# One table of order numbers changed, and 128 transposes of a hybrid GLA / DeltaNet / MLA block written as matrix products

## The reference

```python
g_cum = jnp.cumsum(g, axis=2)
g_h = jnp.swapaxes(g_cum, 2, 3)
incl = jnp.tril(jnp.ones((C, C), dtype=bool))
diff = g_h[..., :, None] - g_h[..., None, :]
decay = jnp.where(incl, jnp.exp(jnp.where(incl, diff, 0.0)), 0.0)
l_strict = jnp.where(strict, jnp.einsum('bnthd,bnshd->bnhts', k_beta, k) * decay, 0.0)
t_inv = lax.linalg.triangular_solve(eye + l_strict, ..., left_side=True, lower=True, unit_diagonal=True)
```

## Time and profile before

| what | value |
|---|---|
| median of three runs | 2180.62 us |
| profiled execution, its own time | 2180.62 us |
| its span (first to last instruction) | 2178.7 us |
| PE busy | 2109.8 us, 97% of the span |
| PEld, DVE, ACT, POOL busy | 1439.6, 927.1, 841.6, 294.7 us |
| mean granted PE clock | 0.991 |

### The profile page before, as it was taken

How to read it: one execution, slowest core, us unless ns; L and a number is a source line. 1 busy time by engine, 2 the same in 40 slices (tenths; PEclk the granted TensorE clock), 3 DMA queues, 4 the chain that set the end, 5 groups by cost and what they waited for, 6 DMA issues and landing times. The chain is left out here.

```text
span 2178.7 us, 31299 instructions
## 1 busy us (share of the span) xinstructions
PE 2109.8 (97%) x10890; PEld 1439.6 (66%) x10890; DVE 927.1 (43%) x2293; ACT 841.6 (39%) x2203; POOL 294.7 (14%) x623
## 2 busy tenths in 40 slices
PE   8999999999989999999999999999989979999998
PEld 5667576656556886555674446776676668976687
DVE  3023554857563235443231111246677653343321
ACT  1223354645443234444231112246556443245420
POOL 1000006153350000000000000000632641000000
PEclk9999999999999999999999999999999999999999
DMA  8326303221311022111122332231422312332333
GB/s 271 105 73 195 118 22 109 65 68 43 100 40 49 26 88 79 60 50 44 63 77 78 116 99 101 77 100 41 134 79 74 97 55 78 108 100 85 112 129 122
DMA packets 192443, 192.31 MB, mean 88 GB/s; under 512 B 28943, under 2 KB 186467, under 8 KB 191779
## 3 DMA queue, kind: packets, MB, share of 16 engines
q1 hardware_dynamic: 186048, 171.08, 25.4%
q0 software_dynamic: 4672, 18.89, 2.8%
q10 hardware_dynamic: 1571, 0.34, 0.1%
HBM read 180.78 MB, written 9.50 MB: 87 GB/s over the span
## 5 line engine op out<-in xcount | busy, mean ns | idle before, releaser
L1153 PE MATMUL bank<-hT,ring 128*128 128x512 f32 (+2 forms) x1856 | 715.1, 533 | 5.6 <-ACT hT L1557 3.6
L1153 PEld LDWEIGHTS bank<-hT,ring 128*128 128x128 f32 (+1 forms) x1856 | 331.7, 189 | 257.1 <-issue 239.1
L1153 PE MATMUL bank<-ring,hT 128*128 128x256 f32 (+2 forms) x2112 | 449.8, 368 | 0.0
L1153 PE MATMUL bank<-WORK 128*128 128x128 f32 (+6 forms) x3056 | 392.0, 286 | 37.3 <-DVE O L2202 13.3
L1153 PEld LDWEIGHTS bank<-ring,hT 128*128 128x128 f32 x2112 | 380.4, 190 | 62.4 <-issue 17.2
L1153 PEld LDWEIGHTS bank<-WORK 128*128 128x128 f32 (+4 forms) x3056 | 320.5, 170 | 144.9 <-issue 123.3
L1153 PE MATMUL bank<-yT,ring 128*128 128x512 f32 (+1 forms) x768 | 270.2, 489 | 0.0
L1153 PEld LDWEIGHTS bank<-yT,ring 128*128 128x128 f32 x768 | 139.2, 191 | 78.7 <-issue 69.7
L2126 DVE SCALAR_TENSOR_TENSOR WORK<-WORK,CW 128x512 f32<-128x512 f32 (+1 forms) x192 | 142.1, 740 | 2.2
L1512 ACT ACTIVATE E<-bank 128x512 f32<-128x512 f32 (+1 forms) x84 | 45.0, 536 | 207.4 <-PE bank L1153 198.2
L1116 POOL TENSOR_TENSOR WORK<-WORK 128x126 f32<-128x126 f32 (+22 forms) x248 | 107.3, 432 | 19.4
(11 more groups left out here) (215 smaller groups left out, 2009.6 us busy)
## 6 DMA issues: line engine op xcount, KB each, us to landing
ring<-in_w_in_dram SPq DMA_DIRECT2D x92, 1024.0 KB, 5.3
ring<-in_w_branch_dram SPq DMA_DIRECT2D x24, 1024.0 KB, 5.1
ring<-in_ada_w_dram SPq DMA_DIRECT2D x18, 1024.0 KB, 7.1
ring<-in_w_out_dram SPq DMA_DIRECT2D x8, 1024.0 KB, 5.1
WORK<-in_ada_w_dram SPq DMA_DIRECT2D x6, 1024.0 KB, 12.6
ring<-in_mla_q_up_dram SPq DMA_DIRECT2D x8, 576.0 KB, 4.1
xs<-yT POOLq DMA_DIRECT2D x2, 2048.0 KB, 7.5
WORK<-LD POOLq DMA_DIRECT2D x16, 256.0 KB, 3.4
```

What stands on the lines that cost most here:

```text
L1153: return nc.tensor.matmul(o, a, b, start=start, stop=stop, skip_group_check=True)
```

## The change

Two edits. The table `AHEAD` has other numbers and fewer kinds: `ga` 1 to 2, `cv` 6 to 5, `go` -4 to -3, `dn` -3 to -1, `abT` -3 to -7, `dw2` -5 to 3, `vz` 4 to 1, `gqk` -1 to 1; and `norm` -2, `vdsilu` -1, `dg` -12, `ge` -1, `dgp` -2 and `out` 1 are gone, which makes them 0.

In `d1`, PE no longer transposes a broadcast column of the running sums `GC` against the identity. It multiplies a broadcast column of `GG` (the log decays before they are summed) with the triangular table, which sums them on the way. The four results, their bank, what reads them and what `d1` waits for stay.

```diff
-AHEAD = {('yT', 1, 0): 0, 'gw': 4, 'ga': 1, 'dnq': 1, 'yT': -1, 'cv': 6, 'ms': 1, 'mkv': 6, 'muk': -6, 'dx6': 3, 'dqkv': 5, 'd1': -1, 'muq': 2, 'dya': 2, 'vdn': -1, 'gv': 4, 'ab': 4, 'go': -4, 'dn': -3, 'mo': -8, 'vdsil2': 0, 'abT': -3, 'sq': -3, 'nx': 3, 'dy6': 3, 'dv': 1, 'dyb': 2, 'mod': 6, 'gatt': -6, 'gx': -4, 'z2': -4, 'sk': -1, 'dw2': -5, 'modT': -2, 'dw': 1, 'd3': 1, 'gb': -2, 'vz': 4, 'lr': -3, 'mqT': 3, 'vgate': -4, 'gqk': -1, 'dsilu': -2, 'norm': -2, 'vdsilu': -1, 'dg': -12, 'ge': -1, 'dgp': -2, 'out': 1}
+AHEAD = {('yT', 1, 0): 0, 'gw': 4, 'ga': 2, 'dnq': 1, 'yT': -1, 'cv': 5, 'ms': 1, 'mkv': 6, 'muk': -6, 'dx6': 3, 'dqkv': 5, 'd1': -1, 'muq': 2, 'dya': 2, 'vdn': -1, 'gv': 4, 'ab': 4, 'go': -3, 'dn': -1, 'mo': -8, 'vdsil2': 0, 'abT': -7, 'sq': -3, 'nx': 3, 'dy6': 3, 'dv': 1, 'dyb': 2, 'mod': 6, 'gatt': -6, 'gx': -4, 'z2': -4, 'sk': -1, 'dw2': 3, 'modT': -2, 'dw': 1, 'd3': 1, 'gb': -2, 'vz': 1, 'lr': -3, 'mqT': 3, 'vgate': -4, 'gqk': 1, 'dsilu': -2}
...
                     for r in range(2):
                         for hh in range(2):
                             u = 2 * r + hh
-                            ins = tr(ps[:, u * P:(u + 1) * P], col(GC, tt, g, u).broadcast_to([P, P]))
+                            ins = mm(ps[:, u * P:(u + 1) * P],
+                                     col(GG, tt, g, u).broadcast_to([P, P]), kc(C_TRI + r * P))
```

## The result

The changed kernel takes 2193.68 us (median of 4 runs, 2192.64 to 2197.02) against 2181.02 us of the kernel before on the same chip (4 runs, 2179.77 to 2182.47). The ratio is 1.0056, 95% interval 1.0043 to 1.0069: 12.2 us slower, 9.4 to 15.0. One run of the kernel before, beside the last experiment, took 4456.07 us and is left out of that ratio. The time forecast was 2188.0, the range 2178 to 2197. The time is in the range and the direction was the likeliest one, but it lies 1.7 us above the upper end of the forecast alone.

A forecast was written before the change was run, and what follows sets the result against it. PE, busy 97% of the span, was taken to bound the kernel. Passes left on the path 8.6, `dw2` -1.2, GLA and `dg` +1.0, rest 0, clock -1.0 make +7.4 on 2180.6: 2188.0 us, range 2178 to 2197.

The forecast's parts named there:

- the forecast alone: Whole kernel: the main forecast without its rivals, 2184.5 to 2192 us, chance 0.56.
- The size of the new `d1`: PE in `d1`: 128 transposes become two-row products of 0.222 us instead of 0.109, adding 14.5 us in all.
- Rival 4: PE in `d1`: a product takes one pass, so the edit costs PE nothing; 2179.4 us, chance 0.04.
- What is hidden: PE holes at the `d2` and `dx`: 5.9 us of added passes are free, 8.6 stay; bounds 4 and 14.5.
- the first clock term: Two half-clock windows behind PE holes: shorter holes bring less time at 1.2 GHz, -1.0 us; bounds -3.8 and +1.7.
- `dw2` earlier: PE's `dy6` of group 2: waits of 1.18 and 2.07 us for ACT go, layer 1's gain is given back; -1.2 us.
- The last square and sum of the layer change stand as they did: Layer change: moving `out` and `norm` leaves these behind the last `out`, at no cost; bounds -2 and +2 us.
- GLA and `dg`: GLA part: `dg` and the gate entries stand closer to their producers, +1.0 us; bounds -1 and +5.
- the third window: Half-clock stretch before the `dx` of (1,3), 8.43 us of PE busy: POOL's landing decides there, so it gives nothing.
- rival 2: `dg` and `ge`: the order costs more, DVE late for `dgp` once per layer plus half clock; 2197 us, chance 0.15.
- Rival 1: DeltaNet groups: POOL's solve or DVE's chain decides in every group, so all 14.5 us fall into holes; 2175.6 us, chance 0.11.
- Rival 3: PE's clock holds behind the first two windows and one more place, 3 to 4 us back; about 2185 us, chance 0.14.

The follow-up runs named there:

- the last experiment: Kernel before with `dw2` early for group 2 alone and 20 gate and `ys` pieces pulled ahead of one `d2` and three `dx`: 2178.19 us, ratio 0.9982.
- the halves of the heads: Two kernels, each the kernel before with the new `d1` in four of the eight heads, with holes or mostly without: 2182.18 and 2188.14 us.
- the early heads: Kernel before with the new `d1` only in heads (0,0), (0,1), (0,2) and (1,0): 2188.14 us, ratio 1.0029.

## Why the prediction was right, and where it was not

1. *The size of the new `d1`.* Right: 128 more rows, 0.222 us for a product, 14.5 us of passes. The rule in the Trainium skill ("TensorE: Matmul & The Clock Gate", section Terms: the transpose mode is four times faster for float32), by which it would have been 41.9 us, does not hold in this kernel. Rival 4 (one pass) is dead.
2. *What is hidden.* Right, and shown: the holes at the `d2` of (0,1), (1,2) and (1,3) went, those of (0,3), (1,1) and the `dx` of group 2 shrank by 0.9 to 1.5 us with the new `d1` alone, and the halves of the heads cost 1.1 and 6.3 us where the count gave 1.8 and 6.5 to 6.8. One bound doesn't come out of its own words: two more hidden pairs, those of (0,2) and (1,0), leave 8.6 - 1.8 = 6.8 us, not 4. With the first clock term the forecast for the new `d1` was 7.6 us; 6.1 was measured.
3. *`dw2` earlier.* The step that failed. The prediction said -1.2 us, bounds 0 and -3.3; alone it is +4.4. It worked out group 2, where -1.5 us was measured (-3.3 to +0.4), and gave that for an entry that moves the copies in all eight groups. The question to ask was what else the copies now stand ahead of on ACT: in groups 0 and 1 of layer 1 that is `dd`, on which the next head's DVE rows wait, and `dyb`. In the changed kernel the two `dy6` wait only 1.06 and 0.70 us, so the entry's share of the 12.2 us is likely smaller than 4.4; it was not measured well enough to say (2.6 us, with overlapping intervals). The give-back at the `dx` of (1,3) was right: 3.94 us with group 2 alone, and 6.01 in the changed kernel, where PE's half clock just ahead of it is 5.00 us instead of 8.48, which brings it another 1.7 us earlier.
4. *"The last square and sum of the layer change stand as they did".* Wrong: PE waits 1.47 us for ACT's square there, and with the two entries back it doesn't. The prediction put this term at 0. What it costs in time is not shown apart from `dw2` and `dn`.
5. *GLA and `dg`.* Taken +1.0, found -0.4 with the rest of the table, with an error of some 3 us. No wait at `dg`. The working was right: between the end of `dgp` and the row that reads `dg` there are 4.7 us now instead of 9. That row still waits, for ACT, and nothing on PE does:
```profile
1475.08 0.22 DVE L2102 SCALAR_TENSOR_TENSOR WORK<-WORK 128x64 f32<-128x64 f32 x1
...
1479.98 0.23 DVE L2106 COPY WORK<-bank 128x64 f32<-128x64 f32 x1 [1.64 <-ACT WORK L1708]
```
6. *The clock.* Taken -1.0, for the first two windows of the earlier trace rows; not shown. With the new `d1` alone PE's half clock behind those two holes is 5.99 and 3.41 us, more in sum than before; in the changed kernel it is 3.41 and none. Such stretches can't be read off one profile: between two executions of one kernel the clock moves the time by more than 1 us (below). That the third window gives nothing was right, as the new `d1` alone showed.
7. *The rivals.* The measured time lies between the forecast and rival 2, 2197, "the order costs more". It is nearer to rival 2 (3.3 us) than to the forecast (5.7). That rival's headline was true, but not its place: it had `dg` and `ge`, which never waited. Rival 1 (the solve paces more than two groups) is excluded by the early heads, which paid for 6.3 of 7.3 us. Rival 3 was right that the clock holds more: its mean rose from 0.9904 (20 runs) to 0.9927 (10) with the new `d1` alone, and to 0.9919 in the changed kernel. Its 3 to 4 us did not come. In the profile of the new `d1` alone the half-clock time that went lies ahead of the `dx` of (1,3), 10.24 us before and 3.41 after, and there it is given back.

The direction was earned by the count of the passes. That the time stayed inside the range was in part luck: its upper end was put at a dearer order, for a reason that did not occur, and it covered a cost of `dw2`, `norm` and `out` and perhaps `dn` that the prediction had not seen. The idle time, forecast to fall by 5 to 9 us, is the number that shows the miss: 4.5 us of it fell with the new `d1` alone and came back with the table.

## What to carry to other kernels

Count added passes by whether PE stands in a hole at that place; the same edit cost 1.1 or 6.3 us by that alone. When one number of an order table moves a step, work it out for every group and layer that it moves, and name on its engine each instruction that it is now ahead of: the two waits that it removed were worth about 1.5 us (the interval reaches 0), and the place ahead of `dd` and `dyb` in the other groups cost about 6 (4.4 + 1.5). Half clock saved just ahead of a wait that another engine ends is not time saved. A hole is filled with free work only as far as the place the work is taken from can spare it.

## What the runs showed of the hardware

One kernel's executions spread with the granted clock: of 25 of the changed kernel, those with a mean clock of 0.994 took 2187.9 to 2189.0 us and those of 0.991 or 0.990 took 2193.8 to 2197.0. A profile of a time near the low end (2189.74 here) then shows half-clock stretches that do not stand for the median. A stretch can also follow a short wait: in the kernel with `dw2` alone PE ran 3.4 us at 1.2 GHz behind a wait of 1.65 us; the kernel before, which did not wait at that place, has no such stretch there. The new table alone has one too, behind 1.66 us. Products in place of transposes did not raise the clock by themselves: in the early heads 64 transposes became products, and the mean granted clock stayed at 0.9903.
